# GLA's output products by alternating heads, and the S5 loop with inputs two pairs ahead and RWKV shifts four states later, in a two-block sequence model on one core

## The reference, cut to what matters

```python
h = rms_norm_2(x, norm_mix[l])
p_rw, p_s5, p_gla, p_gate = _split(h @ w_in[l], IN_SIZES)
y_rw, y_s5, y_gla = rwkv7_mix(p_rw, ...), s5_mix(p_s5, ...), gla_mix(p_gla, ...)
merged = sum over the branches of gates * (y @ w_branch)

# s5_mix: 32 groups x 64 complex states, one linear recurrence each, then
y = einsum(s_re, c_re) - einsum(s_im, c_im) + d * uf
# gla_mix: 4 chunks of 64 tokens, 4 heads
o = einsum('bhncs,bhnse->bhnce', att, v) + einsum('bhncd,bhnde->bhnce', q_dec, S_prev)
o = o * lax.rsqrt(jnp.mean(o * o, axis=-1) + 1e-5) * norm_g
o = o * silu(go)
# rwkv7_mix begins with a shift by one token, on 1792 columns (14 tiles of 128)
p = p + (_token_shift(p) - p) * mu
```

## Time and profile before

| | us |
|---|---|
| median of three runs (1863.04 to 1865.59) | 1863.68 |
| the profiled execution: its time | 1865.38 |
| the profiled execution: its span | 1863.3 |
| TensorE busy, of the span | 1762.5 |
| VectorE busy | 907.1 |
| ScalarE busy | 406.9 |
| GpSimd busy | 296.3 |

### The profile page before, as it was taken

How to read it: one execution, slowest core, us unless ns; L and a number is a source line. 1 busy time by engine, 2 the same in 40 slices (tenths; PEclk the granted TensorE clock), 3 DMA queues, 4 the chain that set the end, 5 groups by cost and what they waited for, 6 DMA issues and landing times.

```text
span 1863.3 us, 25925 instructions
## 1 busy us (share of the span) xinstructions
PE 1762.5 (95%) x10464; PEld 1393.5 (75%) x10464; DVE 907.1 (49%) x1729; ACT 406.9 (22%) x772; POOL 296.3 (16%) x305
## 2 busy tenths in 40 slices
PE   7999999899999999899899998988999899999997
PEld 5434454488888888656799996866798687888886
DVE  1247542454675444475587654177721432255511
ACT  1312552222002210336222002221421101200000
POOL 0100361022002211005144010066000000000000
PEclk9999999999999999999999998899999999999999
DMA  7874472132233222421354544233312343244443
GB/s 288 308 289 192 148 273 80 46 136 90 94 133 113 91 91 78 171 77 60 115 179 160 173 167 158 91 113 114 114 50 90 123 151 133 91 158 158 143 151 113
DMA packets 38703, 256.22 MB, mean 138 GB/s; under 512 B 4128, under 2 KB 7328, under 8 KB 9024
## 3 DMA queue, kind: packets, MB, share of 16 engines
q1 hardware_dynamic: 36240, 240.86, 36.4%
q0 software_dynamic: 1776, 9.57, 1.4%
q10 hardware_dynamic: 576, 4.19, 0.5%
HBM read 247.27 MB, written 7.34 MB: 137 GB/s over the span
## 4 chain that ended last, share of the span: by engine, by line
PE 80%; DVE 11%; ACT 3%; POOL 2%; issue 2%; DMA 2%; SPq 0%; ACTq 0%; DVEq 0%; POOLq 0%
PE ps L614 79%; DVE arena L1902 1%; PE ps L812 1%; DMA ring<-weights 1%; DVE arena L2058 1%; POOL aux L1705 1%; DMA xT<-x_t 1%; DVE aux L1931 0%; DVE arena L1932 0%; DVE arena L1933 0%; ACT hT L1350 0%; DVE spare L2170 0%; POOL aux L1688 0%; DVE ring L1974 0%; POOL hT L1748 0%
## 5 line engine op out<-in xcount | busy, mean ns | idle before, releaser
L614 PE MATMUL ps<-hT,ring 128*128 128x256 f32 (+3 forms) x3184 | 739.0, 390 | 19.2 <-issue 7.4
L614 PEld LDWEIGHTS ps<-hT,ring 128*128 128x128 f32 (+1 forms) x3184 | 571.4, 193 | 177.2 <-issue 108.4
L614 PE MATMUL ps<-arena,ring 128*128 128x256 f32 (+3 forms) x1884 | 380.2, 358 | 6.0 <-DVE arena L1933 4.2
L614 PEld LDWEIGHTS ps<-arena,ring 128*128 128x128 f32 (+1 forms) x1884 | 317.7, 190 | 59.7 <-issue 13.3
L1688 POOL TENSOR_TENSOR aux<-aux 128x256 f32<-128x256 f32 (+1 forms) x46 | 49.7, 1080 | 611.6 <-ACT aux L1285 543.6
L614 PE MATMUL ps<-arena,sums 128*128 128x256 f32 (+1 forms) x768 | 136.5, 327 | 1.3 <-DVE aux L1997 1.3
L614 PEld LDWEIGHTS ps<-arena,sums 128*128 128x128 f32 x768 | 118.2, 191 | 12.3 <-DVE aux L1997 2.5
L1285 ACT ACTIVATE aux<-xT 128x256 f32<-128x256 f32 (+1 forms) x64 | 31.0, 494 | 285.7 <-DVE xT L2088 93.3
L1705 POOL TENSOR_SCALAR aux<-aux,small 128x512 f32<-128x512 f32 (+1 forms) x48 | 71.0, 1486 | 107.4 <-DVE small L1949 106.9
L614 PE MATMUL ps<-hT,sums 128*128 128x128 f32 (+1 forms) x512 | 79.4, 304 | 1.8 <-DVE arena L1997 1.4
L1724 POOL TENSOR_TENSOR arena<-arena 128x256 f32<-128x256 f32 (+1 forms) x32 | 27.0, 843 | 336.9 <-ACT arena L1471 336.9
(11 more groups left out here) (335 smaller groups left out, 1823.0 us busy)
## 6 DMA issues: line engine op xcount, KB each, us to landing
ring<-weights SPq DMA_DIRECT2D x224, 1024.0 KB, 4.8
kept_turns<-aux ACTq DMA_DIRECT2D x4, 1024.0 KB, 5.6
arena<-kept_turns POOLq DMA_DIRECT2D x6, 512.0 KB, 4.3
kept_keys_values<-spare POOLq DMA_DIRECT2D x1, 2048.0 KB, 8.2
arena<-kept_keys_values POOLq DMA_DIRECT2D x1, 2048.0 KB, 8.1
tab<-tables SPq DMA_DIRECT2D x1, 1344.0 KB, 13.8
arena<-mem_t SPq DMA_DIRECT2D x2, 512.0 KB, 5.7
xT<-ctx_t SPq DMA_DIRECT2D x1, 1024.0 KB, 9.1
```

What stands on the lines that cost most here:

```text
L614: ins = nc.tensor.matmul(o_, lhsT, rhs, start=start, stop=stop, skip_group_check=True)
```

## The change

It does six things. PE issues the inputs of the first two pairs ahead of GLA's output, and each later pair's inputs two pairs ahead, right behind `s5_out`, between two fillers. The run pool is divided: the inputs have four banks (`state`), everything else on PE two, until the loop ends. GLA's output alternates between the two halves of the partitions at each product and lies in the `hold` banks; DVE multiplies it by the gate straight out of PSUM (`gla_gated`) behind tiles 1 and 2, and ACT no longer copies it. The rest of GLA's end (reciprocal and norm) moves from the loop into RWKV's products. DVE shifts RWKV tile n behind tile n+4 instead of behind tile n, with four buffers instead of two, in the space of `sums`, and ACT's Tanh and Sigmoid stand ahead of RWKV's eleventh tile instead of its third. RWKV's page `r_b` moves to the space of `y_rw`.

```diff
+RW_BUFFERS = 4
+RW_LAG = 4
...
+        r_b = y_rw
...
                 for n in (2 * m, 2 * m + 1):
                     taken(pe, ("s5in", n // 4))
-                    open_bank(("bu", n))
+                    open_bank(("bu", n), "state")
...
+            at_run = turn["run"] % len(pools["run"])
+            oldest_first = pools["run"][at_run:] + pools["run"][:at_run]
+            pools["state"], pools["run"], turn["run"] = oldest_first[:4], oldest_first[4:], 0
             s5_in(0)
+            s5_in(1)
             taken(pe, ("gatt",))
             for i in range(2):
                 taken(pe, ("gu", i))
             for hh in range(2):
-                hp = slice(64 * hh, 64 * hh + 64)
-                key = ("go", hh)
-                o_ = open_bank(key)
-                for i in range(2):
-                    for c in range(NCH):
-                        cc = slice(c * CHUNK, (c + 1) * CHUNK)
-                        oo = o_[:, i * T + c * CHUNK:i * T + (c + 1) * CHUNK]
-                        mm(oo, g_vt[hp, i, c, :], g_att[hp, i, cc], True, c == 0)
-                        if c:
-                            mm(oo, g_s[hp, i, c, :], g_qd[hp, i, cc], False, True, key if i == 1 and c == NCH - 1 else None)
+                open_bank(("go", hh), "hold")
+            for i in range(2):
+                for c in range(NCH):
+                    cc = slice(c * CHUNK, (c + 1) * CHUNK)
+                    for part in range(2 if c else 1):
+                        for hh in range(2):
+                            hp = slice(64 * hh, 64 * hh + 64)
+                            key = ("go", hh)
+                            oo = bank(key)[:, i * T + c * CHUNK:i * T + (c + 1) * CHUNK]
+                            lhsT, rhs = (g_s[hp, i, c, :], g_qd[hp, i, cc]) if part else (g_vt[hp, i, c, :], g_att[hp, i, cc])
+                            mm(oo, lhsT, rhs, part == 0, part == 1 or c == 0, key if i == 1 and c == NCH - 1 and part else None)
...
             for hh in range(2):
-                taken(pe, ("go", hh))
+                pe.wait_ge(S["gla_act"], 3 + hh)
                 key = ("gos", hh)
-                o_ = open_bank(key, "hold")
+                o_ = open_bank(key)
...
             for m in range(S5T // 2):
-                if m + 1 < S5T // 2:
-                    s5_in(m + 1)
                 s5_filler(2 * m)
                 s5_out(m)
+                if m + 2 < S5T // 2:
+                    s5_in(m + 2)
                 s5_filler(2 * m + 1)
+            pools["run"], turn["run"] = pools["run"] + pools["state"], 0
...
-                act.wait_ge(S["rw_shifted"], max(i, 1))
+                act.wait_ge(S["rw_shifted"], max(i - RW_BUFFERS + 2, 1))
...
-                did(f(flat2(g_osq, hh), bank(key), ACT.Square))
-                copied(key, flat2(g_o, hh), n=512)
+                did(f(flat2(g_osq, hh), bank(key), ACT.Square), "gla_act", wait=False)
...
-            act.wait_ge(S["rw_shifted"], 1 + RW_FIRST)
-            did(f(r_wg[0:64, 0, :], r_wg[0:64, 0, :], ACT.Tanh), "rw_squash")
-            did(f(r_wg[:, 1, :], r_wg[:, 1, :], ACT.Sigmoid), "rw_squash")
...
             for i in range(RW_FIRST, 14):
+                if i == 10:
+                    act.wait_ge(S["rw_shifted"], 1 + RW_FIRST)
+                    did(f(r_wg[0:64, 0, :], r_wg[0:64, 0, :], ACT.Tanh), "rw_squash")
+                    did(f(r_wg[:, 1, :], r_wg[:, 1, :], ACT.Sigmoid), "rw_squash")
                 rw_tile(i)
...
+            def gla_gated(hh):
+                key = ("go", hh)
+                dve.wait_ge(S["gla_act"], 3 + hh)
+                taken(dve, ("glago", 2 + hh))
+                o_ = bank(key).rearrange("p (a t) -> p a t", a=2)
+                did(tt(y_gla[:, hh:4:2, :], o_, g_go[:, hh:4:2, :], ALU.mult), "gla_dve")
+                did(v.memset(small2[:, 19, 0:1], 0.0), key=key)
+
             def gla_end(hh):
                 taken(dve, ("gos", hh))
-                r = flat2(page(8), hh)
+                r = g_root[:, 2 * hh:2 * hh + 2, :]
                 recip(r)
                 y = y_gla[:, hh:4:2, :]
-                did(stt(y, g_o[:, 2 * hh:2 * hh + 2, :], col("gla_norm_2"), page(8)[:, 2 * hh:2 * hh + 2, :], ALU.mult, ALU.mult))
-                did(tt(y, y, g_go[:, hh:4:2, :], ALU.mult), "gla_done" if hh else None)
+                did(stt(y, y, col("gla_norm_2"), r, ALU.mult, ALU.mult), "gla_done" if hh else None)
...
-                if n < 14:
-                    rw_tile(n)
-                if n in (4, 8):
-                    gla_end(n // 4 - 1)
-                if j == 1 and g:
+                if n in (1, 2):
+                    gla_gated(n - 1)
+                if n >= RW_LAG:
+                    rw_tile(n - RW_LAG)
+                if j == 3 and g:
                     s5_y(g - 1)
+            for i in range(S5T - RW_LAG, 14):
+                rw_tile(i)
...
             plus("qt", c_qt, c_qt)
+            gla_end(0)
             plus("d8", c_b3, eye)
+            gla_end(1)
             plus("r", c_r, c_b3)
```

More of the change, by code:

```diff
@@ L470, in two_blocks @@
         s_s = [y_s5[:, 0:2, :], y_s5[:, 2:4, :], gates[:, 8:10, :], gates[:, 10:12, :]]
-        r_r, r_k, r_v, r_wg, r_lw, r_a, r_g, r_kk, r_b, r_e, r_at, r_kh, r_rt, r_a2, r_k2, r_bon = [page(i) for i in range(16)]
+        r_r, r_k, r_v, r_wg, r_lw, r_a, r_g, r_kk, _, r_e, r_at, r_kh, r_rt, r_a2, r_k2, r_bon = [page(i) for i in range(16)]
         r_vt, r_a2t, r_k2t, r_m2 = [spage(i) for i in range(4)]
+        r_b = y_rw
         r_n1, r_n2 = side_page, r_wg
         c_d, c_dt, c_o, c_d2, c_d2t, c_d4, c_d4t, c_b3, c_qt, c_r = r_lw, r_b, r_e, r_a, r_k, r_r, r_a2, r_k2, r_at, r_kh
-        c_t0, c_t0t, c_e, c_et, c_e2, c_ft, c_tt, c_ie = r_lw, r_b, r_a, r_k, r_r, r_a2, r_k2, r_at
+        c_t0, c_t0t, c_e, c_et, c_e2, c_ft, c_tt, c_ie = r_lw, page(8), r_a, r_k, r_r, r_a2, r_k2, r_at
         r_y = r_kh
+        g_root = page(8)
+        rw_raw = sums[:, :, :, :].rearrange("p a b c -> p (a b c)")[:, 0:RW_BUFFERS * (T + 1)].rearrange("p (n t) -> p n t", t=T + 1)
         r_x = rinv[:, 0:T].rearrange("p (i v) -> p i v", i=4)
@@ L572, in _ @@
             uses = [0] * 8
-            turn = {"run": 0, "hold": 0, "mod": 0}
+            turn = {"run": 0, "hold": 0, "mod": 0, "state": 0}
             pools = {"run": [0, 1, 2, 3, 4], "hold": [5, 6], "mod": [7]}
@@ L1095, in head_sums @@
                     o_ = open_bank(key)
-                    mm(o_[:, :], table("headones"), src[:, 2 * half:2 * half + 2, :].rearrange("p a t -> p (a t)"), True, True,
-                       key)
+                    mm(o_.rearrange("p (a t) -> p a t", a=2), table("headones"), src[:, 2 * half:2 * half + 2, :], True, True, key)
             gate_tiles(2)
@@ L1547, in rw_tile @@
                 did(f(page(n // 4)[:, n % 4, :], bank(key)[:, 0:T], ACT.Copy, scale=small2[:, 17, n:n + 1]))
-                did(f(raw[:, i % 2, 1:T + 1], bank(key)[:, 0:T], ACT.Copy, scale=col("rw_mu_2", 0, n)), key=key, wait=False)
+                did(f(rw_raw[:, i % RW_BUFFERS, 1:T + 1], bank(key)[:, 0:T], ACT.Copy, scale=col("rw_mu_2", 0, n)), key=key, wait=False)
             gate_n = iter(range(24))
@@ L1570, in _ @@
             for hh in range(2):
-                rooted(("gos", hh), flat2(page(8), hh), 1.0 / GDV, "eps5")
-            act.wait_ge(S["rw_shifted"], 1 + RW_FIRST)
-            did(f(r_wg[0:64, 0, :], r_wg[0:64, 0, :], ACT.Tanh), "rw_squash")
-            did(f(r_wg[:, 1, :], r_wg[:, 1, :], ACT.Sigmoid), "rw_squash")
+                rooted(("gos", hh), flat2(g_root, hh), 1.0 / GDV, "eps5")
             def gelu(g):
@@ L1580, in _ @@
             for i in range(RW_FIRST, 14):
+                if i == 10:
+                    act.wait_ge(S["rw_shifted"], 1 + RW_FIRST)
+                    did(f(r_wg[0:64, 0, :], r_wg[0:64, 0, :], ACT.Tanh), "rw_squash")
+                    did(f(r_wg[:, 1, :], r_wg[:, 1, :], ACT.Sigmoid), "rw_squash")
                 rw_tile(i)
             gates_(GATE_EARLY)
-            act.wait_ge(S["gla_done"], 1)
+            act.wait_ge(S["gla_dve"], 5)
             for n in range(4):
@@ L1622, in _ @@
                     product("t0", c_t0)
+                    act.wait_ge(S["gla_done"], 1)
                     product("t0t", c_t0t)
@@ L1639, in _ @@
             for half in range(2):
-                rooted(("rv", half), flat2(r_b, half), 1.0 / RD, "epsgn")
+                rooted(("rv", half), flat2(r_a, half), 1.0 / RD, "epsgn")
             table_of(ACT.Sqrt)
@@ L2090, in _ @@
             did(ts(small2[:, 17, 0:14], cols("rw_mu_2", 0, 14), -1.0, 1.0, ALU.mult, ALU.add))
-            did(v.memset(raw[:, :, 0:1], 0.0), "rw_shifted")
+            did(v.memset(rw_raw[:, :, 0:1], 0.0), "rw_shifted")
             def rw_tile(i):
@@ L2096, in rw_tile @@
                 dst = page(n // 4)[:, n % 4, :]
-                did(tt(dst, dst, raw[:, i % 2, 0:T], ALU.add), "rw_shifted")
+                did(tt(dst, dst, rw_raw[:, i % RW_BUFFERS, 0:T], ALU.add), "rw_shifted")
```

(4 more changed lines are left out.)

## The result

The changed kernel takes 1840.01 us in the median of four runs (1838.61 to 1840.90). The kernel before, run beside it, took 1864.63 us (1863.04 to 1867.19). The ratio is 0.986, with a 95% interval from 0.9847 to 0.9873. The forecast was 1841 us, in a range from 1835 to 1852. The span fell from 1863.3 to 1837.4 us.

What follows compares the result with a forecast made beforehand. PE, busy 95% of the span, was taken as the bound. Savings 13.6 + 3.9 + 1.4 + 4.3 + 0.9 - 1.1 = 23.0 us from 1865.38 give 1842.4; corrected for the median, 1841 us, range 1835 to 1852.

Steps and rivals of the forecast that it cites:

- Waits and clock of the loop: S5 loop: all PE waits for POOL go, 13.6 us, and the slow clock behind them, 3.9 us.
- adjacent fillers: S5 loop on PE: seven fillers directly follow another, each saving 0.2 us, 1.4 us in all.
- What the waits came from: S5 loop: PE's 13.6 us of waits blamed on DVE, ahead of POOL, waiting 24.1 us for ACT's copies.
- the circle: S5 loop: shift needs RWKV tile, PE makes it behind an output needing POOL, POOL needs DVE's next tile; 13.6 us.
- GLA's output: Ahead of the loop on PE: alternating halves takes 5.0 us instead of 9.27, gaining 4.3 us.
- Three projections: Behind GLA's output on PE: 10.95 us instead of 11.86 if the clock holds, gaining 0.9 us.
- New bank waits: Between projections and loop: sums and fillers share two banks, so PE waits for ACT; costs 1.1 us, bounds 0 and 3.
- The second pair's inputs: Ahead of GLA's output on PE: input of pair 1 issued there, priced at 1.06 us.
- GLA's end in RWKV's products: Reciprocals moved into gaps there cost nothing, 0.8 us left; rival that they are uncovered: at most 8.4 us, chance 0.07.
- DVE and POOL as the bound: Rival in the S5 loop: shifts and POOL operations beside them lose 0.9 us each; 1842 to 1848 us, chance 0.12.

Runs made afterwards that it cites:

- the last experiment: The changed kernel with GLA's two sums of squares in the hold banks instead of the two run banks: 1838.22 us, ratio 0.9849.

## Why the prediction was right, and where it was not

The stretch, in steps: before 111.33; with GLA's output alone 104.43 (-6.9); with GLA's end moved as well, and the pools and buffers, 94.28 (-10.1); with the lag 89.34 (-4.9); with inputs two pairs ahead 84.75 (-4.6). The parts don't add up in another order: two pairs ahead without the lag costs 7.2 instead of giving 4.6, and GLA's end in the loop costs 6.5 with the lag and up to 10.1 without (that step has other parts too).

**Waits and clock of the loop** (17.5 us) and **adjacent fillers** (1.4): right. All waits for POOL went, the clock is 1.00, and the loop takes 67.62 us where 67.6 was forecast.

**What the waits came from**: this step failed in its reason. The prediction wrote of the waits "That is a circle: the shift behind state tile n needs RWKV tile n", and gave GLA's end no part in them. The runs and their traces show three causes. GLA's end: with it in the loop and the circle cut, waits of 4.75 us are there; with it out and the circle whole, 6.3 are left of 13.8. The circle: at most 3.4 of these 6.3. And single shifts of DVE that POOL holds up, 3.13 and 3.52 us instead of 0.42, behind which PE waits 2.88 and 2.41 us. The view that misled was the sum of DVE's waits, 24.1 us: 15.4 of it, which the prediction counted in, lie ahead of the loop, and only 8.6 in it. The earlier trace rows had the hint: two long waits, each behind one reciprocal. The change removes the first two causes, and no shift over 1.53 us is left in its trace, so the sum came out right. What keeps the third away there, the inputs' lead or the places where POOL happens to issue its DMAs, was not tried.

**GLA's output** (4.3 us): the mechanism was right, its size was not. "I take 0.09 a MATMUL" measured 0.058, below the lower bound of 0.064 as well, and the gain was 9.27 - 3.27 = 6.0. The bound was read too high: 24 MATMULs in 1.53 us include the step to the next work, 0.2 us, and the single starts of those products lie 0.102 and 0.007 us apart by turns, 0.055 in the mean, though they stream twice the columns. They, too, change halves only at every second MATMUL. So this was no reason to take more than their price: what it costs, the 0.105 us of the MATMUL that stays in its half, is in both.

**Three projections** (0.9 us): 12.07 - 10.46 = 1.6. The prediction's 11.86 stopped 0.21 us ahead of the next product, so that this piece was in none of its terms. And the projections gain from standing side by side, which the sum took at 3.65 each.

**New bank waits** (-1.1 us): from the first sum to the first filler 3.39 us, where 2.2 + 1.1 = 3.3 was forecast. The two waits, 0.36 and 0.90, are at ACT's copy and ACT's root as described, and the last experiment takes them away.

**The second pair's inputs**: costed at 1.06 us ahead of GLA's output, and free.

With these the stretch's 26.6 us are accounted for: 6.0 for GLA's output and 1.6 for the projections; -1.2 from the first sum to the loop (2.18 us before, 3.39 after); 20.2 in the loop (87.81 to 67.63), of which 1.06 is the input that left it. The prediction's 23.0 was 3.6 short of that: 1.7 in GLA's output, 0.7 in the projections, 1.1 for the input, 0.1 in the rest. The work ahead of the stretch and behind it took 0.2 and 0.4 us more, so the profiled spans differ by 25.9, and the medians by 24.6, with runs of one kernel 2 to 4 us apart. That the forecast lies within 1.0 us of the median is therefore partly luck: by stretches it was 3.6 us too high.

**GLA's end in RWKV's products**: hidden, as forecast. DVE's timeline in the changed kernel, and PE's next products that use `r`:

```profile
1341.24 3.35 DVE L2069 RECIPROCAL arena<-arena 128x512 f32<-128x512 f32 x1
1344.63 0.75 DVE L2164 SCALAR_TENSOR_TENSOR xT<-xT,vec,arena 128x512 f32<-128x512 f32 x1
1352.77 0.69 DVE L2268 TENSOR_TENSOR arena<-ps,tab 128x512 f32<-128x512 f32 x1 [7.39 <-PE ps L619]
...
1354.43 3.35 DVE L2069 RECIPROCAL arena<-arena 128x512 f32<-128x512 f32 x1
1357.82 0.75 DVE L2164 SCALAR_TENSOR_TENSOR xT<-xT,vec,arena 128x512 f32<-128x512 f32 x1
1358.60 1.42 DVE L2268 TENSOR_TENSOR arena<-ps,arena 128x512 f32<-128x512 f32 x2
```

```profile
1360.90 3.95 PE L619 MATMUL ps<-arena 64*64 64x64 f32 x128
```

The idle time behind the first product is 7.39 us, what 11.57 leaves when 4.14 are filled, to 0.04. `r`'s additions end at 1360.02, and PE's products start at 1360.90 without a wait: 0.9 us to spare, 0.8 by forecast.

**DVE and POOL as the bound**: this rival stayed out, but its price is real. In the changed kernel a shift took 1.53 us at 1221.50, 0.01 us behind the start of POOL's first operation. At 1226.75 the shift began first: it took 0.42 us, and POOL's operation 1.54 instead of 1.26. The Trainium skill (SBUF — State Buffer, Who interferes with whom) says that such a pair excludes each other, and the trace agrees. The prediction's price of 0.9 us fits the usual case, but not the largest: the blocked shifts of 3.13 and 3.52 us in the experiments with inputs one pair ahead lost 2.7 and 3.1. POOL still ended its last tile at 1275.94, 2.7 us ahead of the last output at 1278.63; the forecast was 1276.3.

## What to carry to other kernels

A long wait in a loop may have several causes that cover each other. Remove each alone, measure the stretch, and look for single instructions that are much longer than their like, before the largest number in a table of waits is taken for the reason; and see first where in the window that number's waits stand. If one product's weights lie in the upper half of the rows and the next one's in the lower, alternate them product by product. A change of order that leaves less work between a producer and its consumer needs slack for the producer in the same step, as the lag was here. And when a pool of banks is divided, count who uses the scarce ones: the two sums of squares didn't need them.

## What the hardware showed that was not expected

Small products on rows that no other used were free here: 16 MATMULs with 32 rows of weights on four groups took 1.09 us, 8 on two groups 1.06. Products with 64 rows, both halves by turns, took 0.058 us each, one half at a time 0.115 at a clock of 0.92. A MATMUL in the other half of the rows, and the other bank, started 0.007 us behind the one before it, one in the same half 0.105.

The clock fell without any gap. With GLA's products in one half at a time PE is shown as busy throughout, and the granted clock still went to 0.50 for over 6 us, into full projections behind them. A fall also followed waits, but not each: behind waits of 2.01, 2.83, 2.88, 3.01 and 3.40 us it came, behind 1.96 and 2.41 it did not, and of two waits of 2.77 and 2.72 us with two buffers only the first was followed by slow products (a filler of 5.41 us, then one of 3.72). What decides this the runs don't show. They show the price: 1.65 us behind the wait of 3.40, and 3.2 us behind each of those of 2.83 and 3.01.

A shift with two inputs in SBUF that met POOL took from 0.42 to 3.52 us. The two longest began while POOL issued DMAs and ended 0.3 us behind its next two operations. At 1239.82 in the changed kernel a shift began beside such an issue as well and took 0.42; what parts the two cases is not shown.
